# Moving small pieces of a hybrid decoder step: value products in two halves, one tile moved, cache shifts re-dealt, four gather banks

## What is computed

```python
h = rms_norm(x)
z = h @ w_in[l]                     # one projection for all branches
# A: dilated window attention, 3 head groups; sample tokens read cached keys and values
# B: gated linear attention (GLA);  C: gated DeltaNet (GDN), solved in chunks
merged = g_a * (o_a @ wb[0]) + g_b * (o_b @ wb[1]) + g_c * (o_c @ wb[2])
x = x + merged @ w_out[l]
x = x + channel_mixer(rms_norm(x))  # layer 0: dense SwiGLU; layer 1: 2 of 8 experts
new_buf = k_all[:, k_all.shape[1] - Wb:]   # caches shifted by one row, for 8 samples, 3 windows
```

## Time and profile before

| | |
|---|---|
| median of 3 runs | 1951.61 us (1945.20 to 1957.02) |
| profiled execution, whole | 1947.83 us |
| its span, first to last instruction | 1946.0 us |
| mean granted TensorE clock | 0.979 |
| TensorE busy | 96% of the span |
| DVE, ACT, POOL busy | 27%, 19%, 7% |
| HBM traffic | 547.74 MB read, 196.63 MB written |

### The profile page before, as it was taken

How to read it: one execution, slowest core, us unless ns; L and a number is a source line. 1 busy time by engine, 2 the same in 40 slices (tenths; PEclk the granted TensorE clock), 3 DMA queues, 4 the chain that set the end, 5 groups by cost and what they waited for, 6 DMA issues and landing times.

```text
span 1946.0 us, 28135 instructions
## 1 busy us (share of the span) xinstructions
PE 1863.8 (96%) x11949; PEld 1293.0 (66%) x11949; DVE 519.7 (27%) x1150; ACT 366.1 (19%) x754; POOL 135.2 (7%) x226
## 2 busy tenths in 40 slices
PE   8999999899899999999999989989699999999998
PEld 5889878786678888788888868747433343433434
DVE  3453532428320000143544243533400000000000
ACT  2231334322010000015124432310110000100101
POOL 3000001203100000000100020320000000000000
PEclk9999999899999999999999989999889999899999
DMA  9842789989489876899759988996629999589993
GB/s 279 260 134 90 264 303 340 305 308 341 149 278 364 300 294 248 309 336 364 265 180 333 320 314 289 361 390 233 239 74 369 368 384 405 217 294 386 373 408 119
DMA packets 254691, 563.84 MB, mean 290 GB/s; under 512 B 11949, under 2 KB 149393, under 8 KB 254288
## 3 DMA queue, kind: packets, MB, share of 16 engines
q1 hardware_dynamic: 235232, 500.14, 71.8%
q0 software_dynamic: 18544, 58.58, 8.9%
q10 hardware_dynamic: 784, 3.25, 0.4%
HBM read 547.74 MB, written 196.63 MB: 383 GB/s over the span
## 4 chain that ended last, share of the span: by engine, by line
PE 91%; DMA 4%; DVE 2%; issue 1%; ACT 1%; POOL 0%; DVEq 0%; ACTq 0%; POOLq 0%
PE PS L866 30%; PE PS L1412 15%; PE PS L793 8%; PE PS L1438 7%; PE PS L1273 4%; PE PS L1313 4%; PE PS L786 3%; PE PS L1287 3%; PE PS L1374 3%; PE PS L910 2%; PE PS L903 2%; DMA arena<-bias_tables 1%; PE PS L1460 1%; PE PS L1244 1%; DMA arena<-in_cache_win_kv 1%
## 5 line engine op out<-in xcount | busy, mean ns | idle before, releaser
L866 PE MATMUL PS<-h,ring 128*128 128x264 f32 x2816 | 653.6, 389 | 0.0
L866 PEld LDWEIGHTS PS<-h,ring 128*128 128x128 f32 x2816 | 527.4, 190 | 106.5 <-issue 21.3
L1577 ACT COPY z<-PS 128x264 f32<-128x264 f32 (+3 forms) x307 | 130.7, 445 | 874.6 <-PE PS L866 527.0
L1412 PE MATMUL PS<-ring,z 128*32 128x512 f32 (+1 forms) x1440 | 212.2, 527 | 1.2 <-ACT z L1577 1.2
L1412 PE MATMUL PS<-arena,z 128*32 128x512 f32 (+1 forms) x1056 | 190.1, 535 | 0.0
L1412 PEld LDWEIGHTS PS<-ring,z 128*32 128x32 f32 x1440 | 68.5, 111 | 126.9 <-issue 111.4
L793 PE MATMUL PS<-h,ring 128*128 128x264 f32 x512 | 115.3, 386 | 1.6 <-DVE h L1965 1.6
L793 PEld LDWEIGHTS PS<-h,ring 128*128 128x128 f32 x512 | 97.2, 190 | 18.6 <-issue 2.0
L1438 PE MATMUL PS<-arena,z 128*32 128x512 f32 x432 | 104.0, 593 | 0.0
L1412 PEld LDWEIGHTS PS<-arena,z 128*32 128x32 f32 x1056 | 55.0, 110 | 53.5 <-issue 53.4
L1273 PE MATMUL PS<-z,ring 128*128 128x264 f32 x384 | 87.3, 388 | 0.0
(11 more groups left out here) (319 smaller groups left out, 1832.3 us busy)
## 6 DMA issues: line engine op xcount, KB each, us to landing
out_win_s<-in_cache_win_kv SPq DMA_DIRECT2D x128, 1023.5 KB, 10.0
ring<-in_w_in SPq DMA_DIRECT2D x88, 1024.0 KB, 6.3
out_win_s<-in_cache_win_kv SPq DMA_DIRECT2D x32, 1022.0 KB, 12.8
ring<-in_moe_w_gate SPq DMA_DIRECT2D x28, 1024.0 KB, 9.2
arena<-in_moe_w_up SPq DMA_DIRECT2D x22, 1024.0 KB, 11.5
ring<-in_moe_w_up SPq DMA_DIRECT2D x22, 1024.0 KB, 8.7
ring<-in_moe_w_down SPq DMA_DIRECT2D x20, 1024.0 KB, 11.3
arena<-in_moe_w_down SPq DMA_DIRECT2D x18, 1024.0 KB, 10.4
```

What stands on the lines that cost most here:

```text
L866: last = mm(bank(l, "p", j)[:, 0:T], w[:, k, P * (j % 2):P * (j % 2) + P], h[:, k, :], start=(k == 0), stop=(k == KT - 1))
L1412: last = mm(m_bank("c", "gu", g, b, w, r)[BLK * j:BLK * j + BLK, 0:n], hs[:, k, P * r + BLK * j:P * r + BLK * j + BLK], v3(slot_ap(set_slo ...
L1577: return nc.scalar.copy(out, in_)
```

## The change

1. `schedule`: six instead of seven tiles behind `gdn_inv`, and one more ahead of `kv_tok`, in both layers. (`64 - 21 - 18 - 16 - 8` is 1.)
2. `mg` goes by quarters (two blocks) instead of halves. `as_v` becomes two steps, one a half. Six blocks of branch 2 stand between them; `as_o` comes directly behind the second, then the last two blocks of branch 2, then branch 0.
3. `SHIFTS`: in layer 0 nothing behind chunks 0 to 23 as before, then two pieces behind every chunk up to 53 (before: up to 45, none behind 46 to 53), one behind each feed-forward chunk as before. In layer 1 two behind chunks 0 to 11 (before 0 to 15), none behind 12 to 23 (before one behind 16 to 23), two behind the rest as before.
4. The gather's tiles go round banks 2, 3, 0, 1 instead of 2, 3.

```diff
-    s += [("gdn_inv", 0), ("gdn_inv", 1)] + p(7)
+    s += [("gdn_inv", 0), ("gdn_inv", 1)] + p(6)
...
-    s += [("kv_tok",), ("att_sc", 0)]
+    s += p(64 - 21 - 18 - 16 - 8) + [("kv_tok",), ("att_sc", 0)]
...
-    s += [("sig", 2), ("as_l",), ("mg", 1, 0), ("as_p",), ("mg", 1, 1), ("as_v",), ("mg", 2, 0), ("as_o",), ("mg", 2, 1)]
-    s += [("mg", 0, 0), ("mg", 0, 1), ("bar", 1), ("wo",)]
+    s += [("sig", 2), ("as_l",), ("mg", 1, 0), ("mg", 1, 1), ("as_p",), ("mg", 1, 2), ("mg", 1, 3), ("as_v", 0)]
+    s += [("mg", 2, 0), ("mg", 2, 1), ("mg", 2, 2), ("as_v", 1), ("as_o",), ("mg", 2, 3)]
+    s += [("mg", 0, q) for q in range(4)] + [("bar", 1), ("wo",)]
...
-            out = [(("gh", 0, d), 2 + d % 2) for d in range(KT)]
+            out = [(("gh", 0, d), (2, 3, 0, 1)[d % 4]) for d in range(KT)]
...
-                    out += [(("gh", 1, d), 2 + d % 2) for d in range(KT)]
+                    out += [(("gh", 1, d), (2, 3, 0, 1)[d % 4]) for d in range(KT)]
...
-            def as_v(l):
-                pe.wait_ge(sems["dd_ready"], V("dd_ready", l))
-                open_bank(pe, l, "rr")
...
-                for m in range(24):
+            def as_v(l, part):
+                if part == 0:
+                    pe.wait_ge(sems["dd_ready"], V("dd_ready", l))
+                    open_bank(pe, l, "rr")
...
+                for m in range(12 * part, 12 * part + 12):
...
-                for d in range(4 * half, 4 * half + 4):
+                for d in range(2 * quarter, 2 * quarter + 2):
...
-SHIFTS = (((24, 0), (46, 2), (CH_MIX, 0), (CH_MIX + CH_FFG + CH_FFD, 1)), ((16, 2), (24, 1), (CH_MIX, 2)))
+SHIFTS = (((24, 0), (CH_MIX, 2), (CH_MIX + CH_FFG + CH_FFD, 1)), ((12, 2), (24, 0), (CH_MIX, 2)))
```

More of the change, by code:

```diff
@@ L197, in mixer_jobs @@
     if k == "as_v":
-        return [("rr",), ("pvs", 0), ("pvs", 1)]
+        return [("rr",)] * (a[0] == 0) + [("pvs", a[0])]
     if k == "as_o":
@@ L201, in mixer_jobs @@
     if k == "mg":
-        return [("mb", a[0], 4 * a[1] + d) for d in range(4)]
+        return [("mb", a[0], 2 * a[1] + d) for d in range(2)]
     if k == "wo":
@@ L1228, in as_p @@
                 last.then_inc(full(l, "pk"), 1)
-            def as_v(l):
-                pe.wait_ge(sems["dd_ready"], V("dd_ready", l))
-                open_bank(pe, l, "rr")
[L1233 to L1237, removed]
-                for m in range(24):
+            def as_v(l, part):
+                if part == 0:
+                    pe.wait_ge(sems["dd_ready"], V("dd_ready", l))
+                    open_bank(pe, l, "rr")
+                    for t in range(4):
+                        last = mm(bank(l, "rr")[:, 32 * t:32 * t + 32], K("hmap", 64)[:, P * t:P * t + P],
+                                  dd.rearrange("p a b -> p (a b)"), start=True, stop=True)
+                    last.then_inc(full(l, "rr"), 1)
+                    wait_read(pe, l, "pk")
+                for m in range(12 * part, 12 * part + 12):
                     hb, g, j = m // 12, m % 12 // 4, m % 4
@@ L1258, in as_o, with mg @@
                 last.then_inc(full(l, "pvo"), 1)
-            def mg(l, b, half):
+            def mg(l, b, quarter):
                 src = [oaT, z[:, Z_BG:Z_BG + 4, :], z[:, Z_CZ:Z_CZ + 4, :]]
@@ L1266, in mg @@
                 ch = [CH0[l] + CH_PROJ + 2 * MERGE.index(b) + q for q in range(2)]
-                if half == 0:
+                if quarter == 0:
                     for n in ch:
                         wait_chunk(pe, n)
-                for d in range(4 * half, 4 * half + 4):
+                for d in range(2 * quarter, 2 * quarter + 2):
                     open_bank(pe, l, "mb", b, d)
@@ L2362, in as_p, with as_v @@
                 ts(dd[:, 3, :], K("bsel", 64), rowinv[0:64, 0:1], None, MUL).then_inc(sems["dd_ready"], 1)
[L2364 to L2370, removed]
+            def as_v(l, hb):
+                if hb == 0:
+                    wait_full(dve, l, "rr")
+                    cp(rrs, bank(l, "rr")[:, 0:P]).then_inc(free(l, "rr"), 1)
+                wait_full(dve, l, "pvs", hb)
+                tt(prod[hb], bank(l, "pvs", hb), K("hmap"), MUL).then_inc(sems["mask_ready"], 1)
+                dve.drain().then_inc(free(l, "pvs", hb), 1)
             def as_o(l):
@@ L2400, in mg @@
                     last = tt(z[:, d, :], z[:, d, :], z[:, 8 + d % 4, :], ADD)
-                if b == MERGE[2] and half:
+                if b == MERGE[2] and quarter == 3:
                     last.then_inc(sems["acc_ready"], 1)
```

## The result

The changed kernel took 1902.91 us, median of 4 runs (1900.0 to 1905.53), against 1953.22 for the kernel before, median of 4 (1945.2 to 1957.02): a ratio of 0.9745, 95% interval 0.9716 to 0.9774, faster by 50 us. In the last set of runs on one chip it took 1903.66 (6 runs) against 1951.48 (11 runs), ratio 0.9766 (0.9741 to 0.9790). The forecast was 1902 with a range of 1889 to 1922. The profiled execution took 1900.0 us with a span of 1898.2, 47.8 less than before; its mean granted clock is 0.991.

A forecast was written before the change was run, and what follows sets the result against it. TensorE, busy 96% of the span, was taken as the bound. Terms of 3.4 + 14.8 + 15.2 + 12.9 = 46.3 us off the profiled 1947.83 gave 1901.5, say 1902, range 1889 to 1922.

The forecast's parts named there:

- Part 1: Solving stretch: with one tile fewer and no shifts there, layer 1's wait on DVE goes; 3.4 us.
- Part 2: Attention start: the extra tile fills idle time and bias tables land sooner; 7.4 us a layer, 14.8 us in all.
- they would meet the weights' small packets: Attention start: with shifts issued at other times, bias tables land at twice the rate; DVE starts 3.8 us sooner.
- the clock need not fall: Behind the attention-start pauses: with only about 2 us of idle time left, the clock stays up, worth some 2 us.
- Part 3: Sample attention's value products in halves: six merge blocks cover the loads; 4.6 us in layer 0, 10.6 in layer 1, sum 15.2.
- Part 4: Gather on four banks: pauses go and the clock stays up; 7.1 plus 5.8, sum 12.9 us; 4.0 if only waits go.
- I leave one at 6.01: Gather group 0: of its last three pairs one stays at 6.01 us; 20.3 us becomes 14.5, a gain of 5.8.
- A: Gather: its 8-row products, not the pauses, keep the clock low; gain 4.0 instead of 12.9, 1910.4 us; chance 0.15.
- B: Attention start: bias tables land no sooner or key stores hold DVE; gain there 7.2, total 1909.1 us; chance 0.12.
- E: More than forecast: layer 0's value loads are not slowed and the attention-start gain reaches its cap; 1894 us; chance 0.07.
- C: End of layer 0's mixer: moved shifts delay output and feed-forward weights, up to 43 us exposed; about 1961 us; chance 0.02.
- D: Pauses only move, for instance to the value products' second half and `att_pv`; 10 us or less gained, 1943; chance 0.03.

The follow-up runs named there:

- banks: The kernel before with only the gather's tiles put on four banks: 1937.99 us, ratio 0.9948.
- split: The kernel before with only the value products in halves and the merge by quarters, cache shifts unmoved: 1928.90 us, ratio 0.9895.
- order: The kernel before with the three matmuls of each gather tile in the order 8, 128, 128 tokens, still two banks: 1949.36 us, ratio 0.9995.
- tile: The kernel before with only one tile moved from the solving stretch to ahead of attention: 1943.49 us, ratio 0.9969.
- shifts: The kernel before with only the new table of cache shifts: 1949.11 us, ratio 1.001.

## Why the prediction was right, and where it was not

The median is right to 1 us, and the sum of the terms to 1.5 us of the span (46.3 against 47.8). Part of that closeness is luck: part 2 gave 3.7 us less than forecast and part 4 gave 5.2 more. Parts 1 and 3 came out within 0.1 us, by the mechanism that was named. Parts 2 and 4 went the way that was forecast and are off in size, each by a step that is named below.

**Part 1** (3.4, measured 3.5): the wait is gone in both layers, the run of tiles takes 23.3 us. DVE's 22.0 after the start of the tiles held in layer 1 too. The text didn't see that the tile alone would have raised the wait to 8 or 9 us, nor that the clock falls behind such a wait; that the two edits come as a pair carried it. The 3.4 also rests on the one profile that it was read from: the other three profiles that have both the old table and the old place of the tile (banks, split, order) wait there 4.26, 5.24 and 5.54 us, and in all three the rows behind ran at the half clock.

**Part 2** (14.8, measured 11.1): the term of 7.4 a layer was too large. The step that failed is the landing of the tables, "they would meet the weights' small packets": POOL's queue did have more of the engines, 0.42 MB from 334 to 336 and 0.58 MB from 338 to 340 against the 0.27 of the earlier trace rows, but DVE started 10.3 us after POOL's issue instead of 12.2, sooner by 1.9 in layer 0 (2.7 in layer 1) and not by 3.8. The text's own numbers don't give 3.8 either: 0.77 MB at 0.13 MB/us are 5.9 us, and twice the rate saves half of that, 3.0; at the 0.21 MB/us that the queue had from 334 to 336 it is an estimated 2.3. The queue's rows in the change, from 338 to 340, answer to the earlier trace rows:

```profile
q0 software_dynamic: 166, 0.58, 75.7%
q1 hardware_dynamic: 178, 0.18, 26.6%
```

Packets of both queues are again about as many, and those of the other queue now carry less, as the prediction's sentence on turns by packet has it.

Nor did "the clock need not fall" hold: in the change the 12 instructions behind the second pause took 2.93 us in both layers, after pauses of 2.04 and 2.16 us in one and 1.05 and 2.16 in the other. It is not the same in every run: of the 18 such places in the nine profiles with the moved tile, 12 read 2.93 and six read 1.57 to 2.86, and 2.93 stands behind a first pause of 0.59 as well. The pause of 1.45 became 2.16 because DVE, once the tables are early, is itself late next; the text had looked for what is late next behind the scores, not among them.

**Part 3** (15.2, measured 15.1): 4.1 and 11.0 against 4.6 and 10.6. The price of 6.0 for the shifts beside layer 0's loads was taken from layer 1. It is 5.98 in the run without them, and 5.2 where the shifts alone were changed. The wait spread over the second run was given as about 8 us in both layers and is 7.0 and 5.7. The Trainium skill's page DMA: Bandwidth & Descriptors, in its section on queues, rings and completion order, has each DMA engine take turns between rings packet by packet. That fits here too: the values end sooner as soon as the shifts' packets are gone (4.4 and 4.0 us). Any other way of sharing the engines would fit as well.

**Part 4** (12.9, measured 18.1): group 1 was right, 7.1 against 7.2. Group 0 was sized at 5.8 and gave 10.9. Two steps failed. "I leave one at 6.01" is one: the three last pairs all ran at 4.26 and gave 6.8. (The list of signs had it right, "seven of 4.3 us"; the sum priced six.) The larger one is that the sum began at the second pair, so what the first pair and the pause behind it could give was put at nothing, without a reason; they gave 4.1. In the profile before, the first pair holds a stall of 1.88 us between two of its instructions that waits for nothing shown. In the profiles this stall is tied to the split: the five kernels without the split (before, banks, tile, shifts, order) have a stall of 1.1 to 2.5 us there, the nine profiles with it have none. What in the split takes it away is open; the banks don't, since with the banks alone it stayed at 1.99. One candidate is left untested: the split changes TensorE's list of instructions, and the views of the DMA queues show loads of instructions within 1.5 us of the gather's start in profiles with the stall and in profiles without, which decides nothing. So these 1.9 us belong to another part of the change than the one they are counted under.

The rivals: A is excluded by the order run and by group 1's clock, 1.00 with the 8-row products still there. B is half true: the tables came sooner, by less. E did not happen. C did not happen: the stage from the output weights on was not longer (275.69 against 275.68). The run with 15 pieces more in that stage shows that it was near: there the mechanism of C cost 17.4 us. D is excluded. The profiled run lies 3 us below its median, and the one before lay 4 below its own; the sum gave 1901.5 for the profiled execution, which took 1900.0, and the median lies 3 above that, so two small differences nearly cancel in 1902 against 1902.9.

The Trainium skill's page TensorE: Matmul & The Clock Gate, in its section on psum-queue depth-cycling, was named for the 12.9, and its section Why this matters for your kernels for the 4.0. The runs side with the first (13.5 us in the profile where the banks alone are taken back), with one limit: behind the same pause of 0.66 us 27 pairs took about 6.0 us and nine took 4.3.

## What to carry to other kernels

Price a move of background transfers by the nearest stage that carries the same load already: layer 1's loads gave layer 0's cost to within 1 us (6.0 against 5.98 and 5.2). Ask of every piece that is displaced where it goes; in both places tried here, layer 0's first chunks and its feed-forward stage, what the holes brought was paid back for the most part or more than in full. Read a wait in more than one profile before it is priced: the one of 3.37 us was 4.3 to 5.5 in three others. Two edits around one wait (work moved away from it, transfers moved away from the engine that ends it) can each be worth little or cost something alone, and should be tried as a pair.

## What the runs showed of the hardware

- After pauses of 0.66 us, one after another in the gather, the granted clock is 1.2 GHz for most pairs and 2.4 GHz for others, with the gather's code the same: 27 pairs of about 6.0 us and nine of 4.3 behind the same pause. Without the pauses it was 2.4 GHz in every profile of group 1.
- A wait of 3.37 us in the solving stretch left the clock up (1.16 us for the eight instructions behind it in the earlier trace rows); waits of 4.26, 5.24, 8.15 and 8.99 us at the same place were followed by 2.07 or 2.08 us for the same eight. At the scores pauses of 0.59 to 2.27 us and of 2.16, close together, were followed by 2.93 us for twelve instructions in 12 of 18 places and by less in the others.
- The stage that waits for twelve loads of 256 KB was 4 to 6 us longer when two shift pieces of 1 MB were queued beside each weight chunk.
